# Four column units of the adaLN modulation move from TensorE's attention steps to VectorE's projection steps

## The reference, cut to what matters

```python
ca = jax.nn.silu(c)                                   # (1, 1024)
for l in range(2):
    mod = ca @ w_ada[l] + b_ada[l]                    # (1, 6144)
    sh1, sc1, gt1, sh2, sc2, gt2 = jnp.split(mod, 6)
    h = rms_norm(x, g_norm1[l]) * (1 + sc1) + sh1
    proj = h @ w_in[l]                                # groups A, B, C, D
    ya, yb, yc, yd = diff_attention(A), neighborhood_attention(B), conformer_conv(C), dilated_attention(D)
    x = x + gt1 * (concat(ya, yb, yc, yd) @ w_out[l])
    h2 = rms_norm(x, g_norm2[l]) * (1 + sc2) + sh2
    x = x + gt2 * hier_moe(h2, ...)                   # 32 experts, 6 MB of weights each
return rms_norm(x, g_final)
```

## Time and profile before

| | |
|---|---|
| median of 3 runs | 1803.88 us (1802.73 to 1806.07) |
| profiled execution, its own time | 1805.69 us |
| span in the profile | 1803.8 us |
| mean granted TensorE clock | 0.973 of full speed |
| TensorE busy | 1589.4 us, 88% |
| VectorE busy | 695.3 us, 39% |
| ScalarE busy | 435.6 us, 24% |
| read from memory | 520.99 MB |

### The profile page before, as it was taken

The page is one execution under the profiler, slowest core; times in us unless marked ns, Lnnn a source line. Parts: engine busy times, 40 slices in busy tenths (PEclk is TensorE's granted clock), DMA queues, the critical chain, the costliest instruction groups (busy, mean ns, idle before and its releaser), DMA issues.

```text
span 1803.8 us, 22591 instructions
## 1 busy us (share of the span) xinstructions
PE 1589.4 (88%) x7494; PEld 763.4 (42%) x7494; DVE 695.3 (39%) x1432; ACT 435.6 (24%) x989; POOL 194.1 (11%) x199
## 2 busy tenths in 40 slices
PE   5999998998998998787889999999899988887883
PEld 2455645453333343333345555455333333333331
DVE  1677576352222112222157855743422222222124
ACT  2111567112111112111121016742111221111111
POOL 0000022111111011111000002101111111111010
PEclk9999999989999999999999999999999999999997
DMA  9625533079999999999972355212799999999994
GB/s 362 231 70 202 195 115 110 17 293 398 407 401 407 408 408 404 417 410 417 365 298 93 122 204 208 68 48 101 290 400 407 403 409 406 411 416 404 399 395 180
DMA packets 118493, 527.56 MB, mean 292 GB/s; under 512 B 16529, under 2 KB 22673, under 8 KB 69265
## 3 DMA queue, kind: packets, MB, share of 16 engines
q1 hardware_dynamic: 100944, 491.49, 69.0%
q0 software_dynamic: 12496, 24.51, 4.2%
q10 hardware_dynamic: 4976, 10.55, 1.6%
HBM read 520.99 MB, written 23.86 MB: 302 GB/s over the span
## 4 chain that ended last, share of the span: by engine, by line
PE 56%; DMA 27%; SPq 6%; DVE 5%; issue 3%; ACT 3%; POOL 1%; ACTq 0%; DVEq 0%; POOLq 0%
DMA ring<-in_w_exp_up 20%; PE ps L1015 18%; PE ps L1373 17%; PE ps L1228 6%; SPq L841 5%; PE ps L1371 4%; DMA hT<-in_w_exp_up 3%; PE ps L1170 2%; PE ps L1184 2%; PE ps L1210 2%; PE ps L1041 1%; DMA ring<-in_w_in 1%; ACT arena L1664 1%; DMA yexp_d<-arena,masks 1%; PE ps L1404 1%
## 5 line engine op out<-in xcount | busy, mean ns | idle before, releaser
L1373 PE MATMUL ps<-ring,arena 128*64 128x512 f32 x1952 | 589.1, 603 | 59.2 <-ACT arena L1664 35.0
L1373 PEld LDWEIGHTS ps<-ring,arena 128*64 128x64 f32 x1952 | 184.8, 138 | 273.5 <-issue 260.2
L1015 PE MATMUL ps<-ring,hT 128*128 128x512 f32 (+1 forms) x768 | 255.0, 487 | 1.5 <-DVE z L1804 0.9
L733 DVE TENSOR_TENSOR arena<-ps,arena 64x512 f32<-64x512 f32 (+1 forms) x64 | 44.3, 693 | 488.6 <-ACT arena L1658 418.6
L1658 ACT ACTIVATE arena<-ps 128x512 f32<-128x512 f32 x64 | 38.2, 597 | 778.9 <-PE ps L1373 724.3
L1015 PEld LDWEIGHTS ps<-ring,hT 128*128 128x128 f32 x768 | 144.4, 191 | 101.5 <-issue 91.2
L1373 PE MATMUL ps<-home,arena 128*64 128x512 f32 x320 | 148.6, 619 | 24.2 <-DMA ring<-in_w_exp_up 20.5
L1373 PE MATMUL ps<-hT,arena 128*64 128x512 f32 x336 | 151.5, 605 | 6.9 <-DMA ring<-in_w_exp_up 6.9
L980 POOL DMA_INDIRECT yexp_d<-arena,masks x64 | 59.3, 927 | 850.3 <-DVE arena L743 772.9
L741 DVE TENSOR_TENSOR arena<-ps,gate 64x512 f32<-64x512 f32 (+1 forms) x64 | 43.7, 683 | 266.2 <-PE ps L1373 246.6
L1228 PE MATMUL ps<-ring,hT 128*128 128x512 f32 x256 | 112.5, 595 | 0.0
(11 more groups left out here) (218 smaller groups left out, 1645.2 us busy)
## 6 DMA issues: line engine op xcount, KB each, us to landing
ring<-in_w_exp_up SPq DMA_DIRECT2D x108, 1024.0 KB
ring<-in_w_exp_down SPq DMA_DIRECT2D x88, 1024.0 KB
ring<-in_w_exp_gate SPq DMA_DIRECT2D x62, 1024.0 KB
ring<-in_w_ada SPq DMA_DIRECT2D x24, 2048.0 KB, 11.1
home<-in_w_exp_gate SPq DMA_DIRECT2D x44, 1024.0 KB
work<-in_w_exp_down SPq DMA_DIRECT2D x40, 1024.0 KB
hT<-in_w_exp_gate SPq DMA_DIRECT2D x22, 1024.0 KB
hT<-in_w_exp_up SPq DMA_DIRECT2D x20, 1024.0 KB
```

The costliest lines, as they stand in the source:

```text
L1015: last = pe.matmul(out, lhs(k), rhs(k), start=(k == 0), stop=(k == n - 1))
L1373: last = [pe.matmul(outs[c][HALF * c:HALF * c + HALF, :], lhs(k)[:, 0:HALF], rhs(c, k), start=(k == 0), stop=(k == n - 1), tile_position=( ...
```

## The change

`ADA_STEPS` is replaced by `LATER_STEPS = [29, 29, 30, 30]`. The four units 6 to 9 of each layer are multiplied and added up over their eight rows on VectorE, as the gate units are, in place in their ring slot. This happens during group B's projections: two units behind the taps of tile 0, one each behind tiles 1 and 2. TensorE adds up the partitions by eight matmuls of one column a unit (`mod_of_sums`), two units in step 29 and two in step 30. `TAPS_FIRST` goes from 16 to 32. A ring slot that held a gate unit is free once VectorE has made its sum, and a slot with one of the four units once `mod_of_sums` has filled its bank.

```diff
-ADA_STEPS = [1, 9, 12, 29]
+LATER_STEPS = [29, 29, 30, 30]
-MOD_LAG = 2
-TAPS_FIRST, TAPS_QK = 16, 5
+TAPS_FIRST, TAPS_QK = 32, 5
-                return l, "mod" if (l, u) in ADA_EARLY[l] else "ada", u
+                return l, "mod" if (l, u) in ADA_EARLY[l] + ADA_LATER[l] else "ada", u
-                if old is not None:
+                if old is not None and ORDER[old][0] == "ada" and ORDER[old][1:] in ADA_EARLY[l]:
+                    sp.wait_ge(early_ready, len(ADA_EARLY[l]) * l + ADA_EARLY[l].index(ORDER[old][1:]) + 1)
+                elif old is not None:
                     await_filled(sp, last_use(old))
+            def mod_of_sums(l, u):
+                key, w, p0 = (l, "mod", u), slot(UNIT["ada", l, u]), HALF * (u % 2)
+                pe.wait_ge(later_ready, len(ADA_LATER[l]) * l + ADA_LATER[l].index((l, u)) + 1)
+                await_free(pe, key)
+                for k in range(KD):
+                    last = pe.matmul(bank(key)[p0:p0 + HALF, k:k + 1], w[:, 0, k:512:KD], C["ones"],
+                                     start=True, stop=True, tile_position=(0, p0))
+                fills(last, key)
                     if i < NU:
                         scores(i)
-                    if ada_at(l, i - MOD_LAG) is not None:
-                        n = ada_at(l, i - MOD_LAG)
-                        mod(*ADA_LATER[l][n], n % 2)
+                    for m, u in mods_at(l, i):
+                        mod_of_sums(m, u)
                     for u in closed_at(i):
                         attend(u)
-                    if ada_at(l, i) is not None:
-                        ada(*ADA_LATER[l][ada_at(l, i)])
...
+                def later_product(i):
+                    unit = UNIT[("ada",) + ADA_LATER[l][i]]
+                    sum_of_rows(unit, slot(unit)[:, 0, :], later_ready)
...
                         if g == "B" and t == 0:
                             tap(2 * TAPS)
+                            for i in range(2):
+                                later_product(i)
...
+                            if 1 <= t <= 2:
+                                later_product(1 + t)
...
-                    if ada_at(l, i - MOD_LAG) is not None:
-                        mod_out(*ADA_LATER[l][ada_at(l, i - MOD_LAG)])
-                    n = ada_at(l, i - 1)
-                    if n is not None and turned_columns(*ADA_LATER[l][n]):
...
-                        ada_turned(*ADA_LATER[l][n], n % 2)
+                    for m, u in mods_at(l, i):
+                        mod_out(m, u)
```

More of the change, by code:

```diff
@@ L261, in plan_banks @@
                     take((l, "meanA", f), (7, 3)[f])
-            if ada_at(l, step) is not None:
-                m, u = ADA_LATER[l][ada_at(l, step)]
-                take((m, "ada", u), 7)
         for t in range(TT + 1):
```

33 lines of the change are left out of this document (13 added, 20 removed).

## The result

The changed kernel takes 1854.35 us (median of four, 1847.22 to 1860.04), against 1804.62 us for the kernel before in the same series: a ratio of 1.027, with a 95% interval from 1.0237 to 1.0303. I had forecast 1832.6 us and a range up to 1841. The direction was right, the time 22 us too low, and the range missed it.

What follows compares the result with a forecast made beforehand. Memory queues bound the expert stages, which start when the output projection ends, so earlier delays pass through. Projections +23.2, late steps +13.1, removed units -7.6 give +28.7 us: median 1832.6, 8-in-10 range 1820 to 1841.

Steps and rivals of the forecast that it cites:

- the stall in A: Projections, group A: sixteen more taps ahead of `mod_out` make TensorE wait for bank 7, 9.3 us a layer.
- The rival with no stall: Group A: the second `early_rows` isn't held up, its bank being freed otherwise; 1809.4 us, chance 6%.
- The clock term: Group A: TensorE works at half clock after its long wait for bank 7, losing 2.9 us a layer.
- The transfers: Ring slots freed later in attention: late transfers fit an empty queue at no cost; without this cover up to 27 us.
- So the price of the new VectorE work in group B is zero: Projections, group B: the new products hide beside eight query-key products of TensorE; uncovered, 6 us for each late product.
- That 0.6 goes: Group B, first mean: TensorE's 0.6 us wait for VectorE disappears in each layer.
- Gains: 0.8 + 2.3 + 1.2 = 4.3: Attention, steps 0 to 28, layer 0: removing old `ada` units and VectorE's rows there saves 4.3 us.
- Sum: 7.1 + 2.0 - 0.6 (the old wait) - 1.85 - 0.2 [...] = +6.4: Attention, steps 29 and 30, layer 0: four one-column units plus waits, less the old unit and wait, add 6.4 us.
- More low clock: Rival: new waits in steps 29 and 30, or missing `ada` in 9 to 12, bring another 2.9 us a layer; 1838.4, 19%.
- step 12 part: Attention, step 12: in the rival with further low clock, no gain from the removed unit there, giving 1842 us.
- No row here shows such a load: Steps 29 and 30: no evidence for a cheaper load, so a one-column unit is priced at 1.77 us.

Runs made afterwards that it cites:

- e1: The kernel before with 32 taps instead of 16 ahead of group A's first query-key tile, nothing else changed; 1826.6 us.
- e9: The kernel before with 32 taps instead of 16, plus 14 idle products in TensorE's wait ahead of group A's tile 2; 1824.6 us.
- e7: The kernel before with two of four units on VectorE, in group B's gaps, one bank, contiguous loads, sums in step 29; 1807.3 us.
- e13: The kernel after with two idle 128x512 products ahead of the turn of attention step 12; 1846.8 us.
- e4: The kernel after with both units of a step written into one filling of bank 7 and read together; 1844.8 us.
- e10: The kernel after with each one-column unit in steps 29 and 30 replaced by three 128x512 products; 1854.7 us.
- e8: The kernel after, unchanged, profiled once more; 1853.3 us.

## Why the prediction was wrong

The forecast was 21.8 us too low. In the profiled execution I expected 1834.4 us and 1847.2 was measured: 12.8 of the miss. The rest is that I put the median 1.8 us below that execution and it lies 7.1 above. The step that failed is the same in most of it: what TensorE's clock does behind its waits in attention. I added a term for it once, behind the stall in A, and none for what the change does to steps 12, 29 and 30.

**Right: the mechanism and size of the stall.** `early_rows` waits 9.62 us by the profile (forecast 9.3), for VectorE's row on `gate`, in both layers, and e1 reproduces it alone. The 0.3 between are the time from the end of `mod_out` to the next `early_rows`: I took it for room and put 0.1, but it is 0.31 before and after. The rival with no stall fell. The clock term had the right sign: 1.9 us by e9, forecast 2.9. I had taken all the work seen at half clock in the earlier trace rows, while here 7 of the 11 us at the lower clock pass in the wait itself. The transfers cost nothing, and the expert stages are as long as before within 2 us.

**Wrong: "So the price of the new VectorE work in group B is zero".** The weights of the first product landed at 172.46, when VectorE had already waited 3.90 us, and not "at about 170, when VectorE is there (169.5)". By that the same bank 7 was late a second time, 1.49 and 1.97 us. I stepped the copies and `centre` through, but not the `mod_out` that stands between the copies of tiles 0 and 1. "That 0.6 goes" was wrong too. Together 2.1 and 2.6 us a layer; less what I had put too high for stall and clock, 0.7, the projections came out 1.3 and 1.9 us over.

**Wrong in size: "Gains: 0.8 + 2.3 + 1.2 = 4.3".** The gain was 1.8 and 1.2 us, together 4.6 less than forecast. I counted the removed units as time given back, at the clock they had run at. In step 9 the unit had been work inside a wait; without it TensorE waits 2.45 us instead of 1.52. And without step 12's unit the lower clock behind that wait lasts longer even where the wait is the old 1.52 us: e7 gains 0.3 and 0.4 instead of 3.5 and 2.5. e13 fills the wait and gets 3.8 and 3.9.

**Wrong in size: "Sum: 7.1 + 2.0 - 0.6 (the old wait) - 1.85 - 0.2 [...] = +6.4".** 9.8 and 9.9. In layer 0 the second unit of a pair starts 2.62 and 2.76 us behind the first; with 1.77 for each second unit that is 8.9, near my 7.1 + 2.0, and less the 2.7 for what went away it is the forecast's 6.3. The missing 3.5 us are the lower clock behind each pair, a term that I had put at nothing (4.2 by the two layers of e4). The rival "More low clock" had it: right steps, 2.9 us a layer, and as cause the waits alone, where e10 and e4 show that wait and one-column matmuls work together. With its step 12 part it gave 1842, still below the result. (For layer 1, without the old wait, the sum's own terms give 7.05 and not 6.7.)

**A row overlooked: the price of a load.** "No row here shows such a load", I wrote of a cheaper one. `attend`'s rows did: 16 loads of 128x64 with neighbouring columns in 1.04 us, against 1.77 for a unit. The 1.77 was right for the strided unit; that a unit could cost half was on record before the change.

**Missed: a forecast of the median from one profile.** The profile before and the median agree within 2 us. Those of the kernel after differ by 7, since each of its waits and narrow runs may or may not bring the clock down, for a shorter or longer time. The profiled execution itself is 41.5 us above before's; 7 to 8 more of the 50 are in executions without a profile. e8 shows such 6 us, and longer low stretches in the same steps; for the one at 1860 us there is only its granted clock of 0.957, so there it stays an inference.

## What to carry to other kernels

Free time on an engine is worth only as much as its queue allows: before work is put ahead of an instruction, look up which bank or buffer that instruction releases and who needs it, and move the release forward first. Taking work from an engine that waits anyway gains little, and on TensorE it can lengthen the wait and the time at the lower clock behind it; in the kernel after, two idle products in that wait were worth more (4.7 us by the rows) than the units removed ahead of them (3.0). When executions of a kernel spread, compare the low-clock stretches of two profiles before believing either.
